# Overflow prepared in its own path, the residual before the last scatter, merged one-hot matmuls, B loaded by ScalarE, and another sequence of 27 expert rounds

## The chip, the cores and the metric

One core of a Trainium2 chip runs the whole kernel, a single program of 14302 instructions. Its engines are TensorE (PE; PEld is its weight load), VectorE (DVE), ScalarE (ACT), GpSimd (POOL) and SyncE (SP, which here only issues transfers and waits). The metric is the device time of one execution in microseconds, the median of the runs shown.

## The reference

One layer of a hybrid backbone in fp32, on 128 context tokens and 256 latent tokens of 1024 channels (384 tokens in all, three tiles of 128):

```
h = RMSNorm(x) * (1 + scale1) + shift1          # six modulation rows = SiLU(cond) @ w_ada + b_ada
p = h @ w_in                                    # S5 input 768 | Fourier input 256 | branch gates 2 x 1024
A = S5(p)                                       # 48 groups of 16 channels, 64 complex states, two directions
B = Re(DFT2(p_f))
x = x + gate1 * ((sig(gA) * (A @ w_proj_s5) + sig(gB) * (B @ w_proj_f)) @ w_out)
h = RMSNorm(x) * (1 + scale2) + shift2
x = x + gate2 * (sum over 6 of 64 experts of gate_e * (silu(h @ w1_e) * (h @ w3_e)) @ w2_e + shared(h))
y = RMSNorm(x) * final_norm_g
```

An expert's three matrices (1024 x 256, 1024 x 256, 256 x 1024) are 1 MB each. `b_re`, `b_im`, `c_re` and `c_im` are the S5 input and output matrices, discretized and raised to powers in the kernel.

## The kernel before

The program is a chain of blocks; all engines meet at the end of each.

**The front.** In the first block SP loads constants and conditioning and then streams 24 weight tiles `w_ada` of 1 MB and tiles of `w_in` through a ring of five places. ACT issues the token tiles and two position tiles (line 340 is the last), then computes SiLU of the conditioning (line 344) and the squares of the norms. POOL issues 16 loads of C (line 277), the two of B (line 280), three small ones, and then computes the powers of C (lines 313 to 317). DVE does the first norm and the S5 parameters (to line 522), waits for B and computes its powers (lines 601 to 603); after the last of them (line 638) ACT copies the modulation rows (line 358) and PE does the lag matmuls (line 478). B's load takes, per part, 48 pieces of 16 numbers (64 B) for each of 128 partitions.

**The expert stage.** Its last block runs all 64 experts once, sorted by their count of tokens. A round takes 128 slots, that is token places, cut in blocks of 32; the kinds of rounds give experts 64, 32 and 32 slots (A), 96 and 32 (B), 128 (C) or 64 and 64 (D). 27 rounds run in seven batches, three rounds in the first and four in each other, in the sequence that `PLAN` writes out by hand. Five expert slots in SBUF form a ring (`sb_W` is the fifth); SP loads the experts in the order of their places: per batch gate and up weights of rounds 0 and 1 (`gate_up`, which waits until PE has used that slot five places earlier), the down weights of round 0 (`downward`, with the like wait), gate_up 2, downward 1, gate_up 3, downward 2, downward 3.

On PE a batch is: gather the slots' tokens by a one-hot matrix S (line 1612), `hidden` of round 0 (line 1575), scatter of the two last rounds of the batch before (line 1547), and then, interleaved, for each round `slot_rows`, `hidden`, `turned` (transposes, line 1582) and `down` (line 1596), with the scatter of rounds 0 and 1 ahead of the down of rounds 2 and 3. After the last batch comes the final scatter. `slot_rows` makes three transposes of S (line 1561) and three matmuls of S with the gates, high and low half, of up to 16 blocks each (line 1563); ACT copies the transposed S (line 1651), DVE sums a slot's two gate halves (`gates`, line 1790), and PE's next `slot_rows` waits for that. DVE further forms gate times SiLU times up (line 1796), the low halves of the down results for the scatter (line 1803), which is exact in two parts, and adds the scatter's banks to the accumulator ACC (line 1741).

Experts that got more tokens than their slots hold are meant to go on in overflow batches, a loop behind a branch on a count (`batches`, line 1456). For that the last batch prepares on DVE: `rounds` (lines 1749 to 1756), 5 x `round_experts` (1758 to 1767), `round_batches` (1769 to 1774), and the first overflow batch's `Tail` (1871 to 1890) and `tail_slots` (1712 to 1721). Here the count is 0, and the loop's body does not run.

After that SP loads X (the tokens before the stage, 1.5 MB, line 1524), two gate rows (`g2b`, line 1526) and the final norm's weight; DVE adds the final scatter, multiplies by the gate and adds X, tile by tile (lines 1905 and 1906), and writes the normed output (line 1915).

## Time and profile before

| | |
|---|---|
| median of 3 runs | 1087.58 us (1085.2 to 1091.76) |
| the profiled execution | 1090.29 us, span 1088.4 us |
| mean granted TensorE clock | 0.93 |
| busy share of the span | PE 85%, PEld 46%, DVE 43%, ACT 17%, POOL 11% |
| bytes moved | 272.52 MB, 250 GB/s over the span |
| first expert load issued | 543.88 us |

Times in rows are microseconds from the start of the span. A line of a timeline has the start, the length, the engine, the line of the kernel, the operation, what is written from what is read, the shape, the number of instructions joined in the line, and in brackets how long the engine had been idle and what released it. An engine with a q (SPq, ACTq) is that engine's issuing part: its line is the issue of a transfer, not its duration. PEclk and the clock are shares of TensorE's full 2.4 GHz.

### The profile page before, as it was taken

How to read it: one execution, taken by the hardware profiler on the slowest of the kernel's cores; microseconds unless marked ns; L12 is line 12 of the kernel's file. 1: busy time of each engine (PE TensorE's matmuls, PEld its weight loads, DVE VectorE, ACT ScalarE, POOL GpSimd, SP SyncE). 2: the span in 40 equal slices, each digit the busy share in tenths (PEclk: the TensorE clock that was granted, in tenths of full speed). 3: DMA queues.
4: the chain of work that ended last, by engine and by line, in shares of the span. 5: the costliest groups of instructions: out<-in, count | busy, mean ns of one | idle time of the engine just before them, and what ended most of it. 6: DMA issues, size and time to landing. Idle time of an engine off the chain costs nothing.

```text
span 1088.4 us, 14302 instructions
## 1 busy us (share of the span) xinstructions
PE 925.6 (85%) x5613; PEld 498.3 (46%) x5613; DVE 470.2 (43%) x1103; ACT 188.3 (17%) x390; POOL 115.3 (11%) x121
## 2 busy tenths in 40 slices
PE   1719609899999899997989999999999999989883
PEld 1204208576557655443654533534535435435342
DVE  4499990125981213324532323223223232232976
ACT  3210001332003300014121111121021111111112
POOL 4599930000000000000000000000000000000000
PEclk9759859799999899997989999999999999989998
DMA  9926503602104471201099989999999999999931
GB/s 294 315 103 232 193 0 118 194 1 79 39 0 187 155 279 58 116 0 58 1 405 387 404 356 428 412 426 425 415 427 425 414 426 427 427 426 395 391 112 64
DMA packets 50364, 272.52 MB, mean 250 GB/s; under 512 B 5755, under 2 KB 14363, under 8 KB 22003
## 3 DMA queue, kind: packets, MB, share of 16 engines
q1 hardware_dynamic: 48694, 267.31, 61.0%
q10 hardware_dynamic: 768, 2.67, 0.8%
q0 software_dynamic: 832, 1.59, 0.6%
q8 instruction: 46, 0.75, 0.3%
q14 instruction: 24, 0.20, 0.0%
HBM read 268.30 MB, written 3.24 MB: 249 GB/s over the span
## 4 chain that ended last, share of the span: by engine, by line
PE 39%; DVE 4%; DMA 3%; issue 2%; ACT 1%; SPq 1%; DVEq 0%
PE bank L1575 16%; PE bank L1596 8%; PE bank L1612 7%; PE bank L1547 6%; DMA sb<-w 3%; PE bank L1582 1%; PE bank L1561 1%; ACT sb_Y L1666 0%; PE bank L1563 0%; DVE sb L1741 0%; SPq L978 0%; DVE sb L1905 0%; DVE sb L1765 0%; DVE sb L1766 0%; DVE sb L1767 0%
## 5 line engine op out<-in xcount | busy, mean ns | idle before, releaser
L1575 PE MATMUL bank<-sb 128*32 128x512 f32 (+2 forms) x1024 | 200.4, 606 | 2.2 <-DMA sb<-w 2.2
L1575 PE MATMUL bank<-sb_W,sb 128*32 128x512 f32 (+1 forms) x448 | 92.8, 644 | 13.2 <-issue 13.2
L1596 PE MATMUL bank<-sb 128*32 128x512 f32 (+2 forms) x512 | 99.3, 598 | 1.1 <-ACT sb L1661 1.1
L749 PE MATMUL bank<-early 128*128 128x384 f32 x256 | 89.7, 499 | 0.0
L1547 PE MATMUL bank<-sb_Y,sb_ST 128*128 128x512 f32 x324 | 83.7, 409 | 3.9 <-DVE sb L1741 2.2
L1575 PEld LDWEIGHTS bank<-sb 128*32 128x32 f32 (+2 forms) x1024 | 56.4, 117 | 66.1 <-issue 66.0
L1741 DVE TENSOR_TENSOR sb<-sb,bank 128x512 f32<-128x512 f32 x84 | 57.7, 687 | 65.2 <-PE bank L1547 64.5
L1612 PE MATMUL bank<-sb_S,sb_H 128*128 128x512 f32 (+1 forms) x336 | 79.3, 396 | 5.3 <-ACT sb_H L1696 4.0
L1612 PEld LDWEIGHTS bank<-sb_S,sb_H 128*128 128x128 f32 x336 | 63.7, 195 | 23.9 <-issue 9.8
L1547 PEld LDWEIGHTS bank<-sb_Y,sb_ST 128*128 128x128 f32 x324 | 55.9, 188 | 36.7 <-DVE sb L1741 14.8
L1803 DVE TENSOR_TENSOR sb_Y<-bank,sb_Y 128x512 fp32r<-128x512 f32 x54 | 37.2, 691 | 71.4 <-ACT sb_Y L1666 71.3
L749 PEld LDWEIGHTS bank<-early 128*128 128x128 f32 x256 | 46.9, 191 | 28.9
L1575 PEld LDWEIGHTS bank<-sb_W,sb 128*32 128x32 f32 (+1 forms) x448 | 27.2, 121 | 68.1 <-issue 67.9
L465 PE MATMUL bank<-early 128*128 128x384 f32 x96 | 34.6, 516 | 23.5 <-ACT early L381 23.5
L1666 ACT ACTIVATE sb_Y<-bank 128x512 fp32r<-128x512 f32 x54 | 32.3, 597 | 110.6 <-PE bank L1596 110.6
L1796 DVE SCALAR_TENSOR_TENSOR sb<-sb,bank 128x256 f32<-128x256 f32 x27 | 13.0, 480 | 85.0 <-ACT sb L1657 83.0
L1596 PE MATMUL bank<-sb_W,sb 128*32 128x512 f32 (+1 forms) x224 | 44.6, 610 | 3.2 <-ACT sb L1661 3.2
L1657 ACT ACTIVATE sb<-bank 128x256 f32<-128x256 f32 x27 | 10.4, 385 | 210.3 <-PE bank L1575 210.3
L478 PE MATMUL bank<-sb 128*32 128x128 f32 x192 | 15.1, 305 | 36.6 <-ACT sb L358 36.6
L1783 DVE COPY sb<-bank 128x512 f32<-128x512 f32 (+1 forms) x28 | 18.8, 672 | 55.9 <-PE bank L1612 55.9
L1076 PE MATMUL bank<-sb 128*128 128x512 f32 x96 | 41.5, 593 | 1.7 <-DVE sb L1226 1.7
L1596 PEld LDWEIGHTS bank<-sb 128*32 128x32 f32 (+2 forms) x512 | 26.0, 115 | 29.7 <-issue 28.1
(309 smaller groups left out, 1214.2 us busy)
## 6 DMA issues: line engine op xcount, KB each, us to landing
sb<-w SPq DMA_DIRECT2D x156, 1024.0 KB, 17.3
sb_W<-w SPq DMA_DIRECT2D x36, 1024.0 KB, 15.4
early<-w_ada SPq DMA_DIRECT2D x24, 1024.0 KB, 13.8
early<-w_in SPq DMA_DIRECT2D x12, 1024.0 KB, 10.0
sb<-w_out SPq DMA_DIRECT2D x1, 4096.0 KB, 16.0
sb<-ada_dram SPq DMA_DIRECT2D x8, 512.0 KB, 13.8
early<-w_proj_s SPq DMA_DIRECT2D x1, 2560.0 KB, 15.9
early<-w_glu SPq DMA_DIRECT2D x1, 2304.0 KB, 9.9
```

What stands on the lines that cost most here:

```text
L465: ins = nc.tensor.matmul(bank[3 + f % 2][:, 0:TOK], w_a[c][:, f * P:(f + 1) * P], hT[:, c, :], start=c == 0, stop=c == KC - 1)
L478: ins = nc.tensor.matmul(bank[kk_bank[f % 3]][32 * q:32 * q + 32, c0:c0 + P], Cpad[:, r, dq, :], BP[:, r, dq].rearrange("p s h -> p (s h)" ...
L749: ins = nc.tensor.matmul(bank[m % 2][:, 0:TOK], w[:, c, P * (m % 2):P * (m % 2) + P], hT[:, c, :], start=c == 0, stop=c == KC - 1)
L1076: ins = nc.tensor.matmul(bank[4 + n][:, :], GLT[:, m, j * P:(j + 1) * P], w_o[:, m, 512 * n:512 * n + 512], start=m == 0, stop=m == KC - 1)
L1547: ins = nc.tensor.matmul(bank[m % 2][:, :], ST[:, p, j * P:(j + 1) * P], YR[:, x, p % 2, 512 * h:512 * h + 512], start=p == ps[0] and x == ...
L1575: ins = nc.tensor.matmul(bank[2 + p % 2][c0:c0 + w, :], XT[:, c, P * p + c0:P * p + c0 + w], slot13[k][:, :, c, :], start=c == 0, stop=c = ...
L1596: ins = nc.tensor.matmul(bank[y_bank[p][h]][c0:c0 + w, :], hidT[:, f, c0:c0 + w], slot2[k][:, f, 512 * h:512 * h + 512], start=f == 0, sto ...
L1612: ins = nc.tensor.matmul(bank[c % 2][:, 0:B.slots], part[:, j, c * P:(c + 1) * P], S[:, j, 0:B.slots], start=j == 0 and x == 0, stop=j == ...
L1666: nc.scalar.activation(YR[:, 0, p % 2, 512 * h:512 * h + 512], bank[y_bank[p][h]][:, :], ACT.Copy).then_inc(y_high, 1)
L1741: tt(ACC[:, j, 512 * h:512 * h + 512], ACC[:, j, 512 * h:512 * h + 512], bank[m % 2][:, :], ALU.add).then_inc(acc_ok, 1)
L1783: nc.vector.tensor_copy(XT[:, c, 0:B.slots], bank[1][:, 0:B.slots]).then_inc(xt_dve, 1)
L1803: tt(YR[:, 1, p % 2, cols_], bank[y_bank[p][h]][:, :], Y[:, 0, p % 2, cols_], ALU.subtract).then_inc(y_low, 1)
```

## The change

- `PLAN` gives the 27 rounds another sequence; the kinds and how many there are of each stay.
- The loads of B go from POOL's queue to ACT's, behind the position tiles, and the scratch for transfers that POOL describes goes from 8192 to 4096 bytes.
- Overflow: counting (`rounds`, `round_batches`) is in batch 1, ahead of its first gates. The rest (which experts, the slots, clearing ACC) is done behind the branch, in functions that only run if the count is over 0.
- `slot_rows`: three matmuls of 160 columns take the place of three transposes and three of the gates. `sb_g` holds, per token tile, twice (16 gates and half of the identity); each matmul writes two groups of 80 columns of bank 7. ACT copies the six identity parts, and DVE's `gates` sums six numbers a slot, not two. The identity is written once, ahead of the first slots.
- Residual: X, the gate rows and the norm's weight lie in the fifth expert slot. X and the weight are loaded once that slot's last expert has been through `hidden`, the gate rows once it has been through `down`. DVE then, in the last batch, multiplies the accumulator so far by the gate and adds it to X, one tile ahead of `down(2)`, one ahead of `down(3)` and one behind it; `residual` handles the final scatter's banks alone, by half tiles.

The diff, without the overflow path's own bodies:

```diff
@@ -50,7 +50,7 @@
 N_CONST = 560
 
 KINDS = dict(A=(2, 1, 1), B=(3, 1), C=(4,), D=(2, 2))
-PLAN = ("CAB", "ADAB", "ABAD", "ABAB", "ADAB", "ADAB", "ABDC")
+PLAN = ("BBA", "ADDA", "ACAB", "ABDA", "ACAD", "ADBB", "ABAB")
...
@@ -276,8 +276,6 @@
                         for a in range(2):
                             pool.dma_start(CL[(r * 4 + q) * GH:(r * 4 + q + 1) * GH, :, a * NS:(a + 1) * NS],
                                            v[q, a]).then_inc(s_c, 16)
-                for r, name in enumerate(("b_re", "b_im")):
-                    pool.dma_start(BL[:, r], i[name][0].rearrange("d (q a) n h -> (a n) (d q) h", a=2)).then_inc(s_b, 16)
                 pool.dma_start(g1n, i["norm1_g"][0].rearrange("(p c) -> p c", c=KC)).then_inc(s_dg, 16)
...
@@ -338,6 +336,8 @@
                 x_tile(1)
                 act.dma_start(at(o_H, D), i["k_pos"][0:P, :]).then_inc(s_pos[0], 16)
                 act.dma_start(at(o_H + D, D), i["k_pos"][P:2 * P, :]).then_inc(s_pos[1], 16)
+                for r, name in enumerate(("b_re", "b_im")):
+                    act.dma_start(BL[:, r], i[name][0].rearrange("d (q a) n h -> (a n) (d q) h", a=2)).then_inc(s_b, 16)
                 act.wait_ge(zero_ok, 1)
...
+        GC, GW = 4 * 4, 4 * 4 + P // 2
...
-        sb_g = ctx.enter_context(nc.sbuf_tensor("sb_g", [P, NT * 2 * 2 * BATCH], F32R))
+        sb_g = ctx.enter_context(nc.sbuf_tensor("sb_g", [P, NT * 2 * GW], F32R))
         by_row = lambda v: v.rearrange("p (j n) -> p j n", j=NT)
-        X = by_row(at(o_V, NT * D))
-        g2b = at(o_A, 2 * D).rearrange("p (r n) -> p r n", r=2)
-        fin_g = at(o_A + 2 * D, D)
+        X = by_row(slot[RING - 1][:, 0:NT * D])
+        g2b = slot[RING - 1][:, 4 * D:6 * D].rearrange("p (r n) -> p r n", r=2)
+        fin_g = slot[RING - 1][:, 3 * D:4 * D]
...
-        gahl_t = sb_g[:, 0:48].rearrange("p (j x k) -> p j x k", j=NT, x=2)
-        gahl_b = sb_g[:, :].rearrange("p (j x k) -> p j x k", j=NT, x=2)
+        gates_id = sb_g[:, :].rearrange("p (j x c) -> p j x c", j=NT, x=2)
+        slot_bank = bank[7][:, 0:NT * 2 * GW].rearrange("p (b c) -> p b c", c=GW)
...
+                last = round_of[max(range(RING - 1, E, RING))] + 1
+                sp.wait_ge(h_mm, last)
+                sp.dma_start(X, x2_dram).then_inc(fin_in, 16)
+                sp.dma_start(fin_g, i["final_norm_g"].partition_broadcast(P)).then_inc(fin_in, 16)
+                sp.wait_ge(y1_mm, last)
+                for r in range(2):
+                    sp.dma_start(g2b[:, r, :], ada_dram[r, 5 * D:6 * D].partition_broadcast(P)).then_inc(fin_in, 16)
                 sp.wait_ge(tail_ok, 1)
                 more = sp.value_load(ids[0:1, 0:1], min_val=0, max_val=MAXT // BATCH)
                 with sp.If(more > 0):
+                    sp.wait_ge(tail_ok, 2)
...
-                sp.wait_ge(h_mm, more * 4 + N_ROUNDS)
-                sp.dma_start(X, x2_dram).then_inc(fin_in, 16)
-                for r in range(2):
-                    sp.dma_start(g2b[:, r, :], ada_dram[r, 5 * D:6 * D].partition_broadcast(P)).then_inc(fin_in, 16)
-                sp.dma_start(fin_g, i["final_norm_g"].partition_broadcast(P)).then_inc(fin_in, 16)
...
                     def slot_rows(p):
 
                         wait_last(pe, gate_col_ok, rd(1, p))
                         for j in range(NT):
-                            nc.tensor.transpose(bank[7][:, j * P:(j + 1) * P], S[:, j, P * p:P * p + P].bitcast(F32), ident)
-                        for j in range(NT):
-                            ins = nc.tensor.matmul(bank[7][:, TOK:TOK + width], S[:, j, P * p:P * p + P],
-                                                   gates_r[:, j], start=j == 0, stop=j == NT - 1)
+                            ins = nc.tensor.matmul(bank[7][:, 2 * GW * j:2 * GW * j + 2 * GW], S[:, j, P * p:P * p + P],
+                                                   sb_g[:, 2 * GW * j:2 * GW * j + 2 * GW], start=True, stop=True)
                         ins.then_inc(slot_rows_mm, 1)
...
-                        nc.scalar.activation(ST[:, p], bank[7][:, 0:TOK], ACT.Copy).then_inc(slot_rows_ok, 1)
+                        nc.scalar.activation(ST[:, p].rearrange("p (b c) -> p b c", c=P // 2), slot_bank[:, :, GC:GW], ACT.Copy
+                                             ).then_inc(slot_rows_ok, 1)
...
-                    nc.vector.tensor_copy(gahl_b[:, :, 0, 0:nk], g).then_inc(ga_high, 1)
+                    nc.vector.tensor_copy(gates_id[:, :, 0, 0:nk], g).then_inc(ga_high, 1)
...
+                def round_batches():
+
+                    step(ts(five, iota[0:1, 0:5], float(BATCH), cum_ex[0:1, E - 1:E], ALU.mult, ALU.is_lt))
+                    step(nc.vector.tensor_reduce(n_more, five, AX_X, ALU.add))
+                    nc.vector.tensor_copy(ids[:, 0:1], n_more).then_inc(tail_ok, 1)
...
+                def overflow_first():
+
+                    count = [0]
+
+                    def first_step(ins):
+                        count[0] += 1
+                        ins.then_inc(tail_step, 1)
+                        dve.wait_ge(tail_step, count[0])
+
+                    for m in range(0, MAXT, BATCH):
+                        round_experts(m, first_step)
+                    nc.vector.tensor_copy(ids[:, 1:1 + MAXT], idx_f).then_inc(tail_ok, 1)
+                    for j in range(NT):
+                        ins = nc.vector.memset(ACC[:, j], 0.0)
+                    first_step(ins)
...
+                def before_residual(j):
+
+                    if j == 0:
+                        dve.wait_ge(fin_in, 64)
+                    step(tt(ACC[:, j], ACC[:, j], g2b[:, min(j, 1)], ALU.mult))
+                    step(tt(X[:, j], X[:, j], ACC[:, j], ALU.add))
...
-                            g = gate_t[:, :, 2 * p + a] if B.tail else gate_b[:, :, 4 * p + c0 // SB]
-                            ins = nc.vector.tensor_reduce(gcol[c0:c0 + w, p:p + 1], g[c0:c0 + w], AX_X, ALU.add)
+                            k = 2 * p + a if B.tail else 4 * p + c0 // SB
+                            ins = nc.vector.tensor_reduce(gcol[c0:c0 + w, p:p + 1], slot_bank[c0:c0 + w, :, k], AX_X, ALU.add)
...
                     if not B.first:
                         add(bt, -6)
-                    if B.last:
+                    if not tail and B.b == 1:
                         rounds()
-                        round_experts(0)
+                        round_batches()
                     gates(0)
                     hidden(0)
-                    if B.last:
-                        round_experts(BATCH)
-                        round_experts(2 * BATCH)
                     gates(1)
                     hidden(1)
-                    if B.last:
-                        round_experts(3 * BATCH)
-                        round_experts(4 * BATCH)
-                        round_batches()
-                    if tail:
-                        tail.items()
-                        tail.tile(0)
                     down(0)
                     gates(2)
                     if n_rounds == 4:
                         hidden(2)
-                        if tail:
-                            tail.tile(1)
                         gates(3)
                         down(1)
-                        if tail:
-                            tail.tile(2)
-                            tail.end()
                         next_slots()
                         hidden(3)
                         add(bt, 0)
+                        if B.last:
+                            before_residual(0)
                         down(2)
+                        if B.last:
+                            before_residual(1)
                         down(3)
+                        if B.last:
+                            before_residual(2)
...
+                for x in range(2):
+                    step(ts(gates_id[:, :, x, 0:GC], ident[:, 0:GC].unsqueeze(1).to_broadcast([P, NT, GC]), 0.0, None, ALU.mult))
+                    nc.vector.tensor_copy(gates_id[:, :, x, GC:GW], ident[:, 64 * x:64 * x + 64].unsqueeze(1).to_broadcast([P, NT, P // 2]))
                 block_slots(0)
...
-                    add(n, -6, (2 * j, 2 * j + 1))
-                    if j == 0:
-                        dve.wait_ge(fin_in, 64)
-                    dve.wait_ge(acc_ok, n(12, 2 * j - 3))
-                    step(tt(ACC[:, j], ACC[:, j], g2b[:, min(j, 1)], ALU.mult))
-                    tt(X[:, j], X[:, j], ACC[:, j], ALU.add).then_inc(x3_ok, 1)
+                    for h in range(2):
+                        m, cols_ = 2 * j + h, slice(512 * h, 512 * h + 512)
+                        dve.wait_ge(scatter_mm, n(12, m - 5))
+                        tt(ACC[:, j, cols_], bank[m % 2][:, :], g2b[:, min(j, 1), cols_], ALU.mult).then_inc(acc_ok, 1)
+                        dve.wait_ge(acc_ok, n(12, m - 4))
+                        ins = tt(X[:, j, cols_], X[:, j, cols_], ACC[:, j, cols_], ALU.add)
+                    ins.then_inc(x3_ok, 1)
...
-    nc = bacc.Bacc("TRN2", target_bir_lowering=False, num_devices=1, dynamic_dma_scratch_size=8192)
+    nc = bacc.Bacc("TRN2", target_bir_lowering=False, num_devices=1, dynamic_dma_scratch_size=4096)
```

## Rows read from the trace of the kernel before

**Rows 1.** The page: the span, and the GB/s moved in its 40 slices.

```profile
span 1088.4 us, 14302 instructions
...
GB/s 294 315 103 232 193 0 118 194 1 79 39 0 187 155 279 58 116 0 58 1 405 387 404 356 428 412 426 425 415 427 425 414 426 427 427 426 395 391 112 64
```

**Rows 2.** Timeline of SP's queue (start us, us): the first expert loads.

```profile
543.88 0.84 SPq L978 DMA_DIRECT2D sb<-w  x2
```

**Rows 3.** Time windows: us, busy of PE to POOL, PEclk, DMA share, GB/s.

```profile
42.00:46.00 4.00, 0.32 (x4) 0.00 (x0) 0.00 (x0) 0.00 (x0) 3.61 (x8) 0.50 0.99 201
...
880.00:890.00 10.00, 7.57 (x57) 2.66 (x57) 3.72 (x9) 1.64 (x4) 0.00 (x0) 1.00 1.00 424
...
1030.00:1040.00 10.00, 5.22 (x26) 2.48 (x26) 9.47 (x21) 1.26 (x3) 0.00 (x0) 0.89 0.17 73
```

**Rows 4.** DMA issues: queue, count, KB each, median us to landing.

```profile
sb<-w SPq DMA_DIRECT2D x156, 1024.0 KB, 17.3
...
early<-x_prompt SPq DMA_DIRECT2D x1, 512.0 KB, 3.5
...
sb<-b_re POOLq DMA_DIRECT2D x1, 384.0 KB, 13.0
...
sb<-b_im POOLq DMA_DIRECT2D x1, 384.0 KB, 13.9
```

**Rows 5.** Timeline of DVE, from the last batch to the end.

```profile
1011.55 0.68 DVE L1763 TENSOR_TENSOR sb<-sb 1x512 f32<-1x512 f32 x1
...
1065.96 0.69 DVE L1803 TENSOR_TENSOR sb_Y<-bank,sb_Y 128x512 fp32r<-128x512 f32 x1 [1.03 <-ACT sb_Y L1666]
...
1068.01 0.69 DVE L1741 TENSOR_TENSOR sb<-sb,bank 128x512 f32<-128x512 f32 x1 [1.36 <-PE bank L1547]
...
1080.54 1.23 DVE L1906 TENSOR_TENSOR sb<-sb 128x1024 f32<-128x1024 f32 x1
```

**Rows 6.** Timeline of PE, last two batches ([idle before <-releaser]).

```profile
970.24 6.10 PE L1547 MATMUL bank<-sb_Y,sb_ST 128*128 128x512 f32 x24
...
976.27 3.64 PE L1596 MATMUL bank<-sb 128*32 128x512 f32 x32
...
1008.64 0.49 PE L1561 MATMUL bank<-sb,sb_S 128*128 128x128 f32 x3
...
1008.88 0.49 PE L1563 MATMUL bank<-sb_g,sb_S 128*128 128x32 f32 x3
...
1024.02 8.78 PE L1575 MATMUL bank<-sb 128*64 128x512 f32 x32
...
1038.02 0.90 PE L1561 MATMUL bank<-sb,sb_S 128*128 128x128 f32 x3 [4.78 <-DVE sb L1790]
...
1044.17 7.03 PE L1575 MATMUL bank<-sb 128*128 128x512 f32 x16
```

**Rows 7.** Timeline of all engines, the front.

```profile
2.14 1.19 ACTq L340 DMA_DIRECT2D early<-k_pos  x1
...
9.81 1.28 ACT L344 ACT_TABLE_LOAD   x1 [9.81 <-DMA sb<-c]
...
41.21 0.51 POOL L313 TENSOR_TENSOR sb<-sb 128x192 f32<-128x192 f32 x1 [2.87 <-ACT sb L370]
...
48.07 0.36 DVE L601 TENSOR_TENSOR sb<-sb 128x192 f32<-128x192 f32 x1 [8.74 <-DMA sb<-b_im]
...
144.05 2.00 POOL L317 TENSOR_TENSOR sb<-sb 128x768 f32<-128x768 f32 x1
...
158.95 0.96 DVE L601 TENSOR_TENSOR sb<-sb 128x768 f32<-128x768 f32 x1
...
162.80 2.54 PE L478 MATMUL bank<-sb 128*32 128x128 f32 x18 [36.57 <-ACT sb L358]
```

**Rows 8.** Source view of L1526, the two gate rows before.

```profile
DMA to landing us min/median/max: 7.8/8.5/9.2
```

**Rows 9.** Source view of L683: issue ns min/median/max of 1 MB in 1024 rows.

```profile
L683 SPq DMA_DIRECT2D early<-w_in x8: 540/658/3412, 197.4 to 276.0; - x8
```

More of the change, by code:

```diff
@@ L1454, in column_tiles, with batches @@
             return [(c, wide, *rest) for c0, w, *rest in experts for c in range(c0, c0 + w, wide)]
-        def batches(eng, body):
+        def batches(eng, body, first=None, after=None):
             for b in range(NB):
@@ L1776, in body @@
                 def body(B):
                     bt, rd = B.per_batch, B.per_round
[L1778 removed]
+                    tail = Tail(B.tail_batch) if B.tail else None
                     n_rounds = len(B.rounds)
[L1780 removed]
+                    if tail:
+                        tail.items()
+                        for j in range(NT):
+                            tail.tile(j)
+                        tail.end()
+                        dve.wait_ge(pm_ok, B.tail_batch(1, 1))
+                        tail_slots(bt(1, 1))
```

45 lines of the change are left out of this document (21 added, 24 removed).

## The prediction

> **What bounds the kernel now.** The profiled execution took 1090.29 us for a span of 1088.4 [rows 1]; 1.9 us lie around the span, and it is 2.7 us above the median, 1087.58, to which I apply every difference worked out below.
>
> I read the time windows first, then the DMA issues, then the timelines of PE and DVE at the end, then the front. From 543.88 on [rows 2] the expert stage is a stream of loads: a window in its middle has a DMA share of 1.00 at 424 GB/s while PE is busy for 7.57 of 10 us [rows 3]. 192 loads of 1 MB (64 experts by 3; [rows 4] has 156 of them) are 201.3 MB, at the 427 GB/s of the page's slices [rows 1] 471 us; the stream ends near 1031.7, as the window from 1030 has a share of only 0.17 [rows 3]. Until then work on an engine counts only if it holds the stream up. After it come 57 us in which nothing is loaded but the residual's inputs, and there each step counts whole. In that end, and in the last batch ahead of it, DVE prepares the overflow: 25 look-up steps and 15 of the tiles, each of 512 columns and some 0.7 us [rows 5], 28 us, with counting and slots some 34. PE waits for it: 4.78 us for the gates at 1038.02, and before that its 32 matmuls of a round took 8.78 us at a lowered clock where a later round took 7.03 [rows 6].
>
> The front is a chain too. DVE waits 8.74 us for b_im, so from 39.3, and starts B's powers at 48.07 [rows 7]. PE's lag matmuls at 162.80 have waited 36.57 us for what follows those powers [rows 7], so what moves this chain moves the end one for one.
>
> **The change, part by part.**
>
> *Overflow.* In batch 1 only counting stays, eleven short steps of DVE ahead of the first gates, none wider than a look-up's 0.68 [rows 5]: at most 7.5 us, and as an estimate 3, being an eighth as wide. PE idles for a quarter of a window of that stream [rows 3], so I price it at 0; without that cover it costs 3. In the last batch 34 us of DVE go. The overflow body does not run here in either kernel.
>
> *Sequence of rounds.* The kinds and counts stay, so the bytes and the end of the stream stay at 1031.7; other stalls at batch borders may move it by 5 us either way. What changes is what lies behind the last gate and up load: SP issues gate_up(3), downward(2), downward(3), so there remain 5 down loads (3 experts, then 2), where there were 3. One takes 2.456 us (1 MB at 427 GB/s): the last gate and up weights land at 1031.7 - 12.3 = 1019.4, and with 2 us for the signal and the round before, hidden(3) starts at 1021.4. With the clock lowered, since PE waited for the load, it takes 8.8, not 7.0, and ends at 1030.2; before, it ended at 1051.2 [rows 6]. Then scatter 6.1 and down(2) 3.6 [rows 6]: 1039.9.
>
> *Residual.* SP now loads X and the norm weight after the hidden of round 25 and the two gate rows (512 KB each) after its down, 1039.9. None of this stands ahead of an expert load in SP's order, and X and the norm weight, 2 MB or 4.9 us behind the last load, are in by 1037. For the gate rows the nearest prices are 3.5 us for 512 KB on an idle stream [rows 4] and 9.2 for this pair behind the 1.5 MB of X [rows 8]. I take 3.5, with 1.2 for the second's bytes at 427 GB/s and, as an estimate, 1.1 for the wake-up and two issues: 5.8, so 1045.7; at 9.2 it is 1049.1. DVE stands in that wait with the down parts of rounds 2 and 3 queued behind it, and PE's final scatter waits for these. Then: first tile 2 x 1.23 = 2.5 (1048.2), two halves of 0.69 [rows 5] (1049.6), second tile 2.5 (1052.1), two halves (1053.5). Final scatter: 1.4 for the first bank [rows 5], six banks of 4 matmuls. At full clock these are 1.0 each, and DVE's third tile and residual (2.5, then 4 x 0.69 = 2.8 a tile) end at 1064.4; at half the clock (1.2 of 2.4 GHz), as PE's transposes after its 4.78 us wait took 0.90, not 0.49 [rows 6], in a window whose mean granted clock is 0.89 [rows 3], they are 2.0 each and end at 1066.2. PE will have waited 10 us: I take 1066.2. From the last residual add to the end of the span it was 6.6 us (1081.8 to 1088.4) [rows 1, 5]: 1072.8. So the stage gives 1088.4 - 1072.8 = **-15.6**.
>
> *Merged matmuls.* Three of 32 columns took 0.49 in the trace's overlapping line, with a pitch of 0.11, and so did the three transposes [rows 6]. Three of 160 columns lie between that pitch (-0.33 a round) and a 512-column one, 6.10 / 24 = 0.25 [rows 6] (+0.03). Nearest is a third of the latter way, -0.24: 27 rounds are -6.5 on PE. But the loads set the pace there, so I take 0; the ends are -3, if half of it comes through, and +1 (27 x 0.03). Six values in gates() rather than two, and ACT's strided copy, are under 0.2 a round beside the loads: 0. Filling the identities is some 1 us on DVE when the stage starts, before the first weights have landed (17.3 us [rows 4]): 0.
>
> *B on ScalarE's queue.* POOL spends 13.0 and 13.9 us on landing b_re and b_im and DVE waits for the second. On ACT's queue they are issued at 3.33, right after k_pos (2.14 + 1.19) [rows 7], and could be in before DVE needs them. What is that worth? At most 8.74. But DVE runs beside POOL's powers: POOL's 768-column step takes 2.00 and DVE's 0.96 when alone [rows 7]; of 8.74 us more beside POOL at 2.0 a step, 4.4 steps of 0.96 = 4.2 are gained. Between 4.2 and 8.7 I take 6. The price is on ACT: B is 2 x 6144 pieces of 64 B, and ACT's first computation (9.81) stands behind both issues. No row shows such a load on ACT. If the issue needs no queue room, ACT loses nothing: -6. If ACT is free once b_re is through (3.3 + 13.0 = 16.3), it starts 7 later, DVE's first stage ends at 46.3, and DVE gains only 1.7; POOL's powers, which wait for ACT's copies (41.21), come 7 later too and keep slowing DVE. Nearest to POOL's own landing, I take this: gain and delay cancel, **0**. Both ends beyond it are rivals below. The smaller scratch costs nothing visible: POOL's remaining loads are c's 48 KB and a few rows.
>
> Sum: -15.6 + 0 = **1072.0 us** against the median.
>
> **The rivals.**
>
> *1. B's pieces take turns with the big rows (about 1086).* The transport is full in the front: share 0.99 at 42 to 46, with only 201 GB/s while b_im's pieces are in flight [rows 3]. If ACT is held until both loads are through, at POOL's landings, 3.3 + 13.0 + 13.9 = 30.2, it starts 20 us late: DVE's first stage ends at 59.7, 11.6 after 48.07, and POOL's powers start 20 late. Between these I take +14: 1072 + 14 = 1086. For it: the two landings. Against it: what POOL's queue takes includes the time its own engine needs to write the pieces. The Trainium skill, page "DMA: Bandwidth & Descriptors", section "Queues, rings and completion order", says that each DMA engine goes round its queues by packets; by that rule B's small packets wait their turn behind packets of the weight stream, and the hold is this rival's, not the forecast's. The drop to 201 GB/s agrees with mixed packets; that ACT is held, no row shows.
>
> *2. ACT is held by the count of pieces (about 1102, slower).* The worst issue of 1024 rows held SP for 3.41 us [rows 9]. B has 12 times as many pieces: 12 x 3.41 = 41 us, so ACT is free at 44, 34 late. DVE starts its powers 24 later, POOL 34: I take +30, 1102. It decides once the front is 21 us late, for then the 15.6 are gone and 5.4 more. Against it: the median of those issues was 0.66, and it was the queue behind a filled stream that held the worst.
>
> *3. The stage gives half back (about 1080).* The gate rows land at 9.2 us, the final scatter stays slow in all, and a new stall at a batch border takes 4: -15.6 + 3.4 + 4 = -8. For it: DVE and PE both hang on two short loads. Against it: the loads then have the transport to themselves.
>
> *4. The change does not do what it says,* that is, the overflow path runs: then the time would rise by whole batches. Hidden needs just the matmuls of 27 rounds and the choice of experts is the data's, so nothing but 0.01 is left for it.
>
> **How the numbers follow.** A measurement tells about 0.5%, 5.4 us, from no change: faster is below 1082.1, slower above 1093.0. Forecast 0.50 (1066 to 1078; the front's bounds of -6 and +6), rival 3 0.12, rival 1 0.22, rival 2 0.13, rest (rival 4 in it) 0.03. Faster: 0.50 + 0.12 + 0.04 of rival 1's lower edge = 0.66. Slower: 0.13 + 0.01 = 0.14. Same: 0.20. The range goes down to 1063 (-15.6, the front at -6 and the merged matmuls at -3) and up to 1090, so that it leaves rival 2, rival 1's upper edge and little else out.
>
> **What would show it.** Right: in the last batch no look-ups on DVE, hidden(3) ending near 1030 less the front's shift, a DVE wait of some 5 to 9 us for the gate rows, the last residual add 6.6 before the end; ACT's first computation no later than 17 and PE's lag matmuls near 163. Wrong: ACT's first computation at 30 or later and the lag matmuls past 175 (rivals 1 and 2), a stream that ends past 1036 less that shift, or rounds whose merged matmuls take over 0.7 us.

## The result: no gain, two shifts of opposite sign

The changed kernel takes 1092.07 us (median of 20 runs, 1085.92 to 1108.48) against 1090.2 of the kernel before in as many; the ratio is 1.0026, interval 1.0014 to 1.0038. One run of each kernel was a slow one (1108.48 here, 3194.91 before), and the ratio leaves those out. The changed kernel's profiled execution has a span of 1090.9 us against 1088.4 [rows 1]. I had predicted 1072.0 and a range up to 1090.

Start with where the two kernels stand at the same landmark. SP issues the first expert load, in the timeline of its queue in the changed kernel, 15.4 us later than before [rows 2]:

```profile
559.27 0.84 SPq L978 DMA_DIRECT2D sb<-w  x2
...
1035.02 0.43 SPq L1518 DMA_DIRECT2D sb_W<-x_dram  x1
...
1054.57 0.80 SPq L1522 DMA_DIRECT2D sb_W<-ada_dram  x2
```

From there to the end it is 1090.9 - 559.27 = 531.6 us, before 1088.4 - 543.88 = 544.5. So the expert stage gained 12.9 us, of the 15.6 that I had summed up, and the front lost 15.4, for which I had put 0. The front after, in the timeline of all engines:

```profile
3.29 0.53 ACTq L340 DMA_DIRECT2D sb<-b_re  x1
3.85 27.90 ACTq L340 DMA_DIRECT2D sb<-b_im  x1
5.26 49.39 SPq L257 DMA_DIRECT2D early<-w_ada  x8
...
31.84 1.28 ACT L344 ACT_TABLE_LOAD   x1 [31.84 <-issue]
...
58.28 0.35 DVE L601 TENSOR_TENSOR sb<-sb 128x192 f32<-128x192 f32 x1
...
60.25 0.51 POOL L311 TENSOR_TENSOR sb<-sb 128x192 f32<-128x192 f32 x1 [38.19 <-ACT sb L370]
...
176.69 6.95 PE L478 MATMUL bank<-sb 128*32 128x128 f32 x64 [42.91 <-ACT sb L358]
```

The second of B's loads holds ACT's queue for 27.9 us, and the computation that stands behind it starts at 31.84 instead of 9.81 [rows 7]. DVE no longer waits for B, but it gets to B's powers 10.2 us later (58.28, before 48.07), and the lag matmuls start 13.9 later (176.69, before 162.80) [rows 7].

The end after, on PE, counted in the text from the first expert load so that the front drops out:

```profile
1036.57 8.36 PE L1574 MATMUL bank<-sb 128*32 128x512 f32 x64 [2.81 <-issue]
1044.86 6.08 PE L1551 MATMUL bank<-sb_Y,sb_ST 128*128 128x512 f32 x24
...
1055.50 3.64 PE L1595 MATMUL bank<-sb 128*32 128x512 f32 x32 [0.56 <-ACT sb L1661]
1067.68 3.78 PE L1551 MATMUL bank<-sb_Y,sb_ST 128*128 128x512 f32 x8 [8.54 <-DVE sb_Y L1841]
1074.57 6.52 PE L1551 MATMUL bank<-sb_Y,sb_ST 128*128 128x512 f32 x16 [3.11 <-DVE sb L1933]
```

The last hidden ends at 485.7 (1044.93 - 559.27); before it was 507.3 (1051.2 - 543.88) [rows 6]. Those 21.6 us are the sequence and the missing overflow work together. But PE then stands for 8.54 us ahead of the final scatter and 3.11 inside it, where it stood 1.49 and 1.90 before, in PE's timeline:

```profile
1066.78 4.10 PE L1547 MATMUL bank<-sb_Y,sb_ST 128*128 128x512 f32 x16 [1.49 <-DVE sb_Y L1803]
1072.78 2.14 PE L1547 MATMUL bank<-sb_Y,sb_ST 128*128 128x512 f32 x8 [1.90 <-DVE sb L1741]
```

The timeline of DVE in the changed kernel shows what both waits are for:

```profile
1060.03 1.23 DVE L1805 TENSOR_TENSOR sb<-sb,sb_W 128x1024 f32<-128x1024 f32 x1 [8.37 <-DMA sb_W<-ada_dram]
...
1073.83 0.69 DVE L1933 TENSOR_TENSOR sb<-bank,sb_W 128x512 f32<-128x512 f32 x1 [3.88 <-issue]
...
1083.59 0.69 DVE L1935 TENSOR_TENSOR sb_W<-sb_W,sb 128x512 f32<-128x512 f32 x1
```

The gate rows are issued at 1054.57, behind the down of the fifth slot's last expert, and DVE waits 8.37 us for them with two rounds' down parts behind it. A second stop of 3.88 us, with nothing that the profile shows to wait for, lies at the branch on the overflow count.

### The profile page after: what moved, and what is told of

Its sections match the earlier page's. It is cut to its first block and busy times, and to the rows that moved or that the text cites. A ratio compares the mean times of both kernels' runs of the same rounds, so it can differ in the third digit from the quotient of the medians.

```text
span 1090.9 us, 14089 instructions
## 1 busy us (share of the span) xinstructions
PE 915.7 (84%) x5532; PEld 488.7 (45%) x5532; DVE 447.1 (41%) x1059; ACT 186.2 (17%) x390; POOL 116.8 (11%) x119
## 3 DMA queue, kind: packets, MB, share of 16 engines
q10 hardware_dynamic: 13088, 3.46, 1.6%
## 5 line engine op out<-in xcount | busy, mean ns | idle before, releaser
L1574 PE MATMUL bank<-sb 128*32 128x512 f32 (+2 forms) x1152 | 189.6, 610 | 6.1 <-DMA sb<-w 3.3
L1595 PE MATMUL bank<-sb 128*32 128x512 f32 (+2 forms) x576 | 94.7, 596 | 4.7 <-ACT sb L1661 4.7
L1551 PE MATMUL bank<-sb_Y,sb_ST 128*128 128x512 f32 x324 | 87.4, 423 | 12.1 <-DVE sb_Y L1841 8.5
L1574 PEld LDWEIGHTS bank<-sb 128*32 128x32 f32 (+2 forms) x1152 | 53.1, 116 | 94.6 <-issue 93.6
L1574 PE MATMUL bank<-sb_W,sb 128*32 128x512 f32 (+2 forms) x320 | 89.3, 615 | 4.5 <-DMA sb<-w 4.5
L1551 PEld LDWEIGHTS bank<-sb_Y,sb_ST 128*128 128x128 f32 x324 | 59.0, 197 | 46.2 <-issue 20.3
L1739 DVE TENSOR_TENSOR sb<-sb,bank 128x512 f32<-128x512 f32 x78 | 53.6, 687 | 63.5 <-PE bank L1551 62.9
L478 PE MATMUL bank<-sb 128*32 128x128 f32 x192 | 15.6, 313 | 42.9 <-ACT sb L358 42.9
L1595 PE MATMUL bank<-sb_W,sb 128*32 128x512 f32 (+2 forms) x160 | 43.6, 596 | 2.1 <-ACT sb L1661 2.1
L1595 PEld LDWEIGHTS bank<-sb 128*32 128x32 f32 (+2 forms) x576 | 24.8, 113 | 44.0 <-issue 36.8
L602 DVE TENSOR_TENSOR sb<-sb 128x192 f32<-128x192 f32 (+2 forms) x32 | 40.7, 1272 | 0.0
```

What stands on the lines that cost most here:

```text
L602: step(tt(dest, src[x1], ar, ALU.mult))
L1551: ins = nc.tensor.matmul(bank[m % 2][:, :], ST[:, p, j * P:(j + 1) * P], YR[:, x, p % 2, 512 * h:512 * h + 512], start=p == ps[0] and x == ...
L1574: ins = nc.tensor.matmul(bank[2 + p % 2][c0:c0 + w, :], XT[:, c, P * p + c0:P * p + c0 + w], slot13[k][:, :, c, :], start=c == 0, stop=c = ...
L1595: ins = nc.tensor.matmul(bank[y_bank[p][h]][c0:c0 + w, :], hidT[:, f, c0:c0 + w], slot2[k][:, f, 512 * h:512 * h + 512], start=f == 0, sto ...
L1739: tt(ACC[:, j, 512 * h:512 * h + 512], ACC[:, j, 512 * h:512 * h + 512], bank[m % 2][:, :], ALU.add).then_inc(acc_ok, 1)
```

## The experiments

My theory after this result: B's loads on ACT's queue hold ACT while their pieces take turns with the weight stream, and that alone costs the front what the stage gains. Its rivals: a hold by the count of pieces; other parts of the change in the front; and, for the stage, which of its four edits made the gain. Each kernel was run beside the kernel before on the chip that it ran on; e5 to e8 ran on another chip than the rest, where the kernel before took 1089.82 us, against 1089.31 and 1089.81. Every kernel from e3 on, e4 and e11 aside, has B on SP's queue. Lag matmuls, first expert load and the stage (from that load to the span's end) are from the profiles.

| run | median us | ratio to before (interval) | lag matmuls | first expert load | stage |
|---|---|---|---|---|---|
| before | 1090.2 | | 162.80 | 543.88 | 544.5 |
| changed | 1092.07 | 1.0026 (1.0014 to 1.0038) | 176.69 | 559.27 | 531.6 |
| e1 before, B on ACT | 1102.61 | 1.0125 (1.0108 to 1.0142) | 176.12 | 557.27 | 543.6 |
| e2 changed, B on POOL | 1082.62 | 0.9938 (0.992 to 0.9956) | 167.20 | 548.27 | 533.8 |
| e3 changed, B on SP | 1054.19 | 0.9675 (0.9659 to 0.9691) | 140.26 | 522.21 | 531.8 |
| e4 B on ACT, alone | 1077.62 (one run) | | 163.36 | 543.10 | 532.7 |
| e5 e3, gate rows early | 1050.49 | 0.9611 (0.9554 to 0.9669) | 140.17 | 521.15 | 526.8 |
| e6 e5, other order | 1043.67 | 0.9597 (0.9559 to 0.9634) | 133.21 | 511.27 | 528.0 |
| e7 e3, old sequence | 1053.3 | 0.9674 (0.9627 to 0.972) | 140.31 | 520.48 | 532.3 |
| e8 e3, work put back | 1054.07 | 0.9681 (0.9656 to 0.9707) | 136.53 | 517.00 | 533.6 |
| e9 e6, C's powers held | 1037.31 | 0.9523 (0.9484 to 0.9561) | 123.29 | 507.43 | 528.0 |
| e10 e6, old sequence | 1053.72 | 0.9671 (0.9628 to 0.9714) | 133.97 | 515.13 | 536.2 |
| e11 before, new sequence | 1077.38 | 0.9889 (0.9849 to 0.9928) | 162.12 | 541.67 | 531.0 |
| e12 e3, old slot rows | 1050.84 | 0.9656 (0.9613 to 0.97) | 136.63 | 514.56 | 530.9 |

Changed, e2, e3 and e4 share one stage, and their profiles put it at 531.6 to 533.8, so a difference of some 2 us between two single profiles tells nothing. The front spreads more: e3, e5 to e8, e10 and e12 share one, and its lag matmuls start between 133.2 and 140.3. So the totals of these runs are compared less than their stages.

### The front: e1 to e4

**e1**, the kernel before with this part alone:

```diff
-                for r, name in enumerate(("b_re", "b_im")):
-                    pool.dma_start(BL[:, r], i[name][0].rearrange("d (q a) n h -> (a n) (d q) h", a=2)).then_inc(s_b, 16)
...
                 act.dma_start(at(o_H + D, D), i["k_pos"][P:2 * P, :]).then_inc(s_pos[1], 16)
+                for r, name in enumerate(("b_re", "b_im")):
+                    act.dma_start(BL[:, r], i[name][0].rearrange("d (q a) n h -> (a n) (d q) h", a=2)).then_inc(s_b, 16)
```

> The kernel before with one part of the change alone: B's two loads on ScalarE's queue behind the position tiles. Theory (the front gives the stage's gain back): ScalarE starts at 31 to 32 instead of 9.8, the lag matmuls at 176 to 177 instead of 162.8, the first expert load 15 us later, and the whole is 15 us slower than before, about 1105. Rival (most of the front's shift comes from something else in the change, or is taken up before the expert stage): under 5 us slower.

Measured: 13.3 us slower, the lag matmuls at 176.12, the expert stage as before. In its timeline the front of the changed kernel is there whole:

```profile
3.88 27.21 ACTq L340 DMA_DIRECT2D sb<-b_im  x1
...
31.18 1.28 ACT L344 ACT_TABLE_LOAD   x1 [31.18 <-issue]
```

So this one edit makes the front's loss, and the rival that something else in the change makes it falls.

**e2** moves the two loads back to POOL's queue, with a scratch of 7168 bytes, as much as fits beside the wider `sb_g`:

```diff
+                for r, name in enumerate(("b_re", "b_im")):
+                    pool.dma_start(BL[:, r], i[name][0].rearrange("d (q a) n h -> (a n) (d q) h", a=2)).then_inc(s_b, 16)
                 pool.dma_start(g1n, i["norm1_g"][0].rearrange("(p c) -> p c", c=KC)).then_inc(s_dg, 16)
...
-                for r, name in enumerate(("b_re", "b_im")):
-                    act.dma_start(BL[:, r], i[name][0].rearrange("d (q a) n h -> (a n) (d q) h", a=2)).then_inc(s_b, 16)
...
-    nc = bacc.Bacc("TRN2", target_bir_lowering=False, num_devices=1, dynamic_dma_scratch_size=4096)
+    nc = bacc.Bacc("TRN2", target_bir_lowering=False, num_devices=1, dynamic_dma_scratch_size=7168)
```

> The changed kernel with B's loads back on GpSimd's queue (scratch of 7168 bytes, as much as fits). Theory: the front is that of before (lag matmuls near 163, first expert load near 544), the expert stage keeps its 531.6 us against 544.5, so 13 us faster than before, about 1077, and some 15 faster than the changed kernel. Rival (the stage's gain depends on the later start, or the smaller scratch slows the front): less than 8 us faster than before.

Measured: 6.7 us faster than before, under the 13 expected: the rival's sign, but by the front and not by the stage, which kept its gain (533.8). In the timeline of POOL:

```profile
37.23 0.55 POOL L282 DMA_DIRECT2D sb<-norm_g  x1
48.74 0.84 POOL L283 DMA_DIRECT2D sb<-d_skip  x1 [10.96 <-issue]
49.68 0.52 POOL L313 TENSOR_TENSOR sb<-sb 128x192 f32<-128x192 f32 x1
```

POOL stops 10.96 us more, ahead of a 3 KB load that went straight through before, and C's powers start at 49.68 instead of 41.21 [rows 7]. That the scratch makes this stop, e1 and the changed kernel show: in both B is on ACT's queue, and POOL comes to that load with 8192 bytes of scratch in e1 and 4096 in the changed kernel. From their POOL timelines, in this order:

```profile
11.19 0.86 POOL L281 DMA_DIRECT2D sb<-d_skip  x1
```

```profile
21.19 0.86 POOL L281 DMA_DIRECT2D sb<-d_skip  x1 [9.97 <-issue]
```

The scratch that I had priced at nothing has a price wherever B stays on POOL's queue; the rest of the change takes the room it had.

**e3** puts them on SP's queue, ahead of the 24 `w_ada` tiles.

```diff
+                for r, name in enumerate(("b_re", "b_im")):
+                    sp.dma_start(BL[:, r], i[name][0].rearrange("d (q a) n h -> (a n) (d q) h", a=2)).then_inc(s_b, 16)
                 for n in range(len(items)):
                     load(n)
```

> The changed kernel with B's loads on SyncE's queue, ahead of the stream of w_ada. Theory: ScalarE is free at once (its first computation near 10), B is in by 20 to 32, the VectorE starts B's powers at 39 without a wait, and w_ada comes 10 to 28 us later, which those powers hide: lag matmuls at 156 to 160, total 1070 to 1076. Rival (w_ada's delay ends last): the modulation rows hold up the lag matmuls and the total is 1085 or more.

Measured: 1054.19, better than the theory's best, and the lag matmuls at 140.26 instead of 156 to 160. **e4** leaves B on ACT's queue, but SP waits for it ahead of its first weight tile:

```diff
+                sp.wait_ge(s_b, 32)
                 for n in range(len(items)):
                     load(n)
```

> The changed kernel, B on ScalarE's queue, but SyncE issues no w_ada before B has landed, so B's pieces meet only the small loads and the token tiles. If the hold comes from taking turns with the weight stream, ScalarE's issue of b_im is over in 10 to 18 us instead of 27.9. If it comes from the count of pieces (2.3 ns for each of 12288), it again takes 25 to 28 us.

Measured: the issue of b_im takes 14.60 us. From the timelines of SP in e3 and of ACT in e4, in this order:

```profile
5.66 12.55 SPq L268 DMA_DIRECT2D sb<-b_im  x1
```

```profile
3.77 14.60 ACTq L341 DMA_DIRECT2D sb<-b_im  x1
```

Without the weight stream the same pieces are out in half the time, on either queue, so it is turn-taking and not the count of pieces alone: 12 x 3.41 = 41 us, my rival 2, was nowhere near. The page's table of queues shows what takes turns. In the changed kernel:

```profile
q1 hardware_dynamic: 48694, 267.31, 60.4%
q10 hardware_dynamic: 13088, 3.46, 1.6%
q0 software_dynamic: 608, 0.80, 0.3%
```

ACT's queue (q10) has 13088 packets; e3, with B elsewhere, has 768 there. The 12320 more are B's 12288 pieces of 64 B and a few besides, one packet each. On SP's queue (q1) e3 has as many more, 61014. POOL's queue (q0) carried the same bytes in 832 - 608 = 224 packets. The Trainium skill, page "DMA: Bandwidth & Descriptors", section "Queues, rings and completion order", has each DMA engine go round its queues packet by packet; by that rule every 64 B piece lets a packet of the weight stream pass first, and the trace agrees: 27.9 us beside the stream, 14.6 without it. The trace's records of single packets show the turns themselves. In the changed kernel, from 12 to 28 us, 713 pieces of B went beside 567 packets of 8 KB of the stream. The stream's first five tiles, 640 such packets that fill its ring of five places, were out at 29.67; by then 1265 of B's 12288 pieces had gone, and the other 11023 went in the next 6.4 us. So most of B waited for a pause of the stream, and ACT came free 2 us after that pause began (31.75; in e1 the pause began at 29.08 and ACT came free at 31.09).

e3 also shows that B's arrival was worth more than I allowed. DVE starts the powers at 36.39 there, 11.7 us sooner than before, and the lag matmuls come 22.5 sooner. I had written that of 8.74 us at most 8.7 come through. What else changed is which engine leads. Before, POOL starts its powers 6.9 us ahead of DVE [rows 7]; in e3 DVE leads by 7.2, and its powers take 103.0 us from first to last, before 113.8. From e3's timelines of DVE and of POOL, in this order:

```profile
36.39 0.35 DVE L601 TENSOR_TENSOR sb<-sb 128x192 f32<-128x192 f32 x1
```

```profile
43.59 0.51 POOL L313 TENSOR_TENSOR sb<-sb 128x192 f32<-128x192 f32 x1 [24.37 <-ACT sb L370]
```

### The stage: e7, e8, e11, e12

**e11** is the kernel before with the new `PLAN` alone:

```diff
-PLAN = ("CAB", "ADAB", "ABAD", "ABAB", "ADAB", "ADAB", "ABDC")
+PLAN = ("BBA", "ADDA", "ACAB", "ABDA", "ACAD", "ADBB", "ABAB")
```

and **e7** is e3 with the same two lines the other way round.

> The kernel before with the new sequence of rounds alone. If the preparation of the overflow is what holds up the last rounds, the sequence alone gives 0 to 3 us from the first expert load to the end (542 to 545 instead of 544.5). If the sequence alone makes the gain, 532 to 535.

> The kernel with B on SyncE's queue and the old sequence of the 27 rounds, all else as changed. Theory by my sum (the sequence moves the last hidden ahead by having five down loads behind its weights rather than three): the last hidden ends 5 us later, 3 to 6 us slower than 1054. Rival (the gain is all the overflow's and the residual's): the same within 2 us.

Measured: the sequence alone makes the whole gain (531.0), and without it the rest makes as much (532.3, within the spread of the changed stage). The two are not additive. In e7 the last hidden moves as the theory has it, by 8.2 us rather than 5, but the total as the rival has it. In e11 DVE's overflow work is still there and PE still waits for it, in its timeline:

```profile
1020.44 0.90 PE L1561 MATMUL bank<-sb,sb_S 128*128 128x128 f32 x3 [6.65 <-DVE sb L1790]
...
1034.62 6.08 PE L1547 MATMUL bank<-sb_Y,sb_ST 128*128 128x512 f32 x24
1051.11 4.12 PE L1547 MATMUL bank<-sb_Y,sb_ST 128*128 128x512 f32 x16 [2.21 <-DVE sb_Y L1803]
```

so its last hidden ends at 493.0 from the first load, 7.3 later than in the changed kernel; yet its final scatter starts at 509.4, against 508.4. In e7 the last hidden ends at 493.5 and the final scatter starts at 509.1. What the last hidden gains in the changed kernel, 7 to 8 us over either, is all but lost in the wait for the gate rows: the final scatter starts some 1 us earlier. In e7 that wait is not there: the timeline of its queue and of DVE, in this order, show the rows issued at 1006.74 and used at 1020.45 with no idle time.

```profile
1006.74 0.80 SPq L1522 DMA_DIRECT2D sb_W<-ada_dram  x2
```

```profile
1019.85 0.69 DVE L1739 TENSOR_TENSOR sb<-sb,bank 128x512 f32<-128x512 f32 x1 [0.24 <-PE bank L1551]
1020.45 1.22 DVE L1805 TENSOR_TENSOR sb<-sb,sb_W 128x1024 f32<-128x1024 f32 x1
```

The reason lies in the code: the residual waits for the fifth slot's last expert, place 59. With the old last batch, ABDC, its eight experts are places 56 to 63, and 59 is in its second round; with ABAB there are ten, 54 to 63, and 59 is in the third. The new sequence takes 8 us off the last hidden and hands them to the residual's loads.

**e8** puts DVE's load back into the last batch of e3:

```diff
+                    work = lambda n: [round_experts(BATCH * k, step) for k in range(n)] if not tail and B.last else None
+                    work(1)
                     gates(0)
                     hidden(0)
+                    work(2)
...
+                    work(3)
                     down(0)
```

and one more on each side of `gates(3)` and `down(1)`.

> The kernel with B on SyncE's queue and, in the last batch, VectorE's load of the old overflow preparation put back as eight look-ups of 3.5 us at the places where it stood (their results are not used). Theory (the preparation held up PE): PE waits again for the gates of rounds 2 and 3, and the total rises by 5 to 10 us over 1054. Rival (with the new sequence PE waits for its weights there anyway): under 2 us.

Measured: 533.6, 1.8 more than e3, which is within the spread of that stage, and the same total (1054.07), not the 5 to 10 us more of the theory. PE does wait again, 4.56 us for the gates of round 2, and its last hidden ends 4.4 later (489.7 against 485.3), but the gate rows' wait takes most of it up. In the timeline of its PE:

```profile
992.87 0.93 PE L1562 MATMUL bank<-sb_g,sb_S 128*128 128x160 f32 x3 [4.56 <-DVE sb L1828]
...
1029.60 3.78 PE L1551 MATMUL bank<-sb_Y,sb_ST 128*128 128x512 f32 x8 [8.65 <-DVE sb_Y L1841]
```

**e12** has three transposes and three narrow matmuls again, with ACT's copy and DVE's two-number sum to match:

```diff
                         for j in range(NT):
-                            ins = nc.tensor.matmul(bank[7][:, 2 * GW * j:2 * GW * j + 2 * GW], S[:, j, P * p:P * p + P],
-                                                   sb_g[:, 2 * GW * j:2 * GW * j + 2 * GW], start=True, stop=True)
+                            nc.tensor.transpose(bank[7][:, j * P:(j + 1) * P], S[:, j, P * p:P * p + P].bitcast(F32), ident)
+                        for j in range(NT):
+                            ins = nc.tensor.matmul(bank[7][:, TOK:TOK + 2 * GC], S[:, j, P * p:P * p + P],
+                                                   gates_id[:, j, :, 0:GC], start=j == 0, stop=j == NT - 1)
```

> The kernel with B on SyncE's queue, with the three transposes and three narrow matmuls of the gates again. By my price (merged matmuls hidden under the loads): within 3 us of 531.8 from the first expert load to the end, and 0.55 to 0.75 us instead of 0.46 to 0.57 on PE per round. Rival (they delay the loads through the chain of gates): 5 us or more longer.

Measured: 530.9, against 531.8 with the merged ones: no difference that two profiles could tell. On PE a round's slot rows took 0.74 us from the first start to the last end (971.26 to 972.00), the merged three 0.46 to 0.57.

### Towards a better kernel: e5, e6, e10, e9

**e5** swaps what lies where in the fifth slot, so that only the third tile of X and the norm's weight wait for the down:

```diff
-        X = by_row(slot[RING - 1][:, 0:NT * D])
-        g2b = slot[RING - 1][:, 4 * D:6 * D].rearrange("p (r n) -> p r n", r=2)
-        fin_g = slot[RING - 1][:, 3 * D:4 * D]
+        X = by_row(slot[RING - 1][:, 2 * D:5 * D])
+        g2b = slot[RING - 1][:, 0:2 * D].rearrange("p (r n) -> p r n", r=2)
+        fin_g = slot[RING - 1][:, 5 * D:6 * D]
...
                 sp.wait_ge(h_mm, last)
-                sp.dma_start(X, x2_dram).then_inc(fin_in, 16)
-                sp.dma_start(fin_g, i["final_norm_g"].partition_broadcast(P)).then_inc(fin_in, 16)
-                sp.wait_ge(y1_mm, last)
                 for r in range(2):
                     sp.dma_start(g2b[:, r, :], ada_dram[r, 5 * D:6 * D].partition_broadcast(P)).then_inc(fin_in, 16)
+                sp.dma_start(X[:, 0:2], x2_dram[:, 0:2]).then_inc(fin_in, 16)
+                sp.wait_ge(y1_mm, last)
+                sp.dma_start(X[:, 2], x2_dram[:, 2]).then_inc(s_b, 16)
+                sp.dma_start(fin_g, i["final_norm_g"].partition_broadcast(P)).then_inc(s_b, 16)
```

> The kernel with B on SyncE's queue, and in the fifth slot the gate rows lie where the gate and up weights were, with X from there on: gate rows and two tiles of X are loaded behind the last hidden of that slot, the third tile of X and the norm weight behind its last down. Theory (VectorE's wait of 8.4 us for the gate rows holds up the final scatter): the wait is gone, the final scatter starts 5 to 7 us earlier, and the total falls from 1054 to 1047 to 1050. Rival (the loads hide the wait, or it turns up at X): within 2 us of 1054.

Measured: DVE's wait, 8.68 us in e3, is 0.97, and the stage is 5.0 us shorter (526.8). The direction is the theory's, the size a little less: counted from the first load, the final scatter starts 3.4 us earlier (504.9 against 508.3), not 5 to 7, and the total went down by 3.7, with runs from 1039.86 to 1051.41.

**e6** also changes DVE's order:

```diff
+                        down(2)
                         if B.last:
                             before_residual(0)
-                        down(2)
+                        down(3)
                         if B.last:
                             before_residual(1)
-                        down(3)
-                        if B.last:
-                            before_residual(2)
...
                 residual(1)
+                before_residual(2)
                 output(0)
```

> As the run before it, and VectorE does the low halves of rounds 2 and 3 ahead of the two products and sums that stood before them, and the third tile's product and sum behind the branch on the overflow count. Theory (the branch costs VectorE the 3.9 us in which it stood idle, and PE's final scatter waits for it): branch and products run beside PE's final scatter and its wait for round 3's down, 3 to 6 us less than the run before it. Rival (VectorE's work in sum sets the end, whatever its order): within 1.5 us of it.

Measured: by the total the theory seems right (-6.8), but the stage is not shorter (528.0). The total is the front's: its lag matmuls start at 133.21 where e3's and e5's start at 140.2, with the same front. The rival holds; the order does nothing, and the idle 3.9 us at the branch stay. In e8 DVE stood only 1.63 there, and the timeline names PE's scatter as what ended it. What makes it 3.9 is open, but the traces have a hint: in each of the ten with a stop of 3.9 to 4.2 us, one packet of 8 KB on the instruction queue (q14) starts 1.9 to 2.1 us before DVE goes on, and in e8 none falls into the stop. That points to the fetch of the code behind the branch; no run tests it.

**e10** is e6 with the old sequence, by e7's edit.

> The kernel of the run with gate rows early and the other order, with the old sequence of rounds. With the residual's wait out of the way the sequence should be worth what it moves the last hidden by: 5 to 8 us longer from the first expert load to the end (533 to 536 instead of 528). If the sequence gives nothing even so, within 2 us of 528.

Measured: 536.2, 8.2 us longer, and the last hidden ends 7.6 later (494.5 against 486.9). With the gate rows out of the way the sequence is worth what it moves.

**e9** tests why the front moves by 7 us between profiles of one front. The seven profiles go by DVE's lead over POOL at their first powers: with a lead of 7.1 to 7.3 us (e3, e5, e7) the lag matmuls start at 140.2 to 140.3, with 8.2 to 8.3 (e8, e12) at 136.5 to 136.6, with 8.6 (e6, e10) at 133.2 to 134.0. In these traces DVE and POOL take each other's steps one for one while both do powers, and DVE's 768-column step, 0.96 alone [rows 7], takes 2.1 to 2.4 beside POOL's. e9 is e6 with POOL holding its widest level:

```diff
                     w = max(m, 1)
+                    if m == 4:
+                        pool.wait_ge(bp_ok, 2)
```

In e6's DVE timeline and then in e9's:

```profile
127.81 2.22 DVE L602 TENSOR_TENSOR sb<-sb 128x768 f32<-128x768 f32 x1
130.07 2.11 DVE L603 TENSOR_TENSOR sb<-sb 128x768 f32<-128x768 f32 x1
```

```profile
120.32 0.95 DVE L604 TENSOR_TENSOR sb<-sb 128x768 f32<-128x768 f32 x1
121.30 0.96 DVE L605 TENSOR_TENSOR sb<-sb 128x768 f32<-128x768 f32 x1
```

> The kernel of the run with gate rows early and the other order (B on SyncE's queue), and GpSimd holds its last level of C's powers, 24 steps of 768 columns, until VectorE has done B's powers. Theory (the two engines take each other's steps one for one, so what ends the front is how many of VectorE's wide steps are done beside GpSimd's wide ones): VectorE's last dozen steps take 0.96 us instead of 2.1 to 2.6, the lag matmuls start 10 to 16 us earlier (117 to 125), GpSimd ends near 162 to 166, still inside the block, and the total is 1028 to 1036. Rival (VectorE's wide steps are slow for another reason, or GpSimd then ends the block): within 4 us of 1043.

Measured: 1037.31 (1036.83 to 1038.66), the best here, 4.8% under the kernel before, and just outside both ranges: the theory's time was up to 1036, the rival's from 1039. The lag matmuls start at 123.29, as the theory has it. That is 10 us sooner than e6, of which 3.8 reach the expert stage, because, as the rival has it, POOL now ends the block:

```profile
123.29 5.87 PE L480 MATMUL bank<-sb 128*32 128x128 f32 x64 [15.40 <-ACT sb L360]
...
159.63 1.80 POOL L319 TENSOR_TENSOR sb<-sb 128x768 f32<-128x768 f32 x1
...
162.05 6.06 PE L706 MATMUL bank<-sb,early 128*48 128x128 f32 x28 [8.01 <-PEq L239]
```

The Trainium skill, page "SBUF — State Buffer", section "SBUF: two separate sides", says that the two engines share a port pair that one step locks whole; the steps' times agree with it: DVE's 2.11 and 2.22 us in e6, beside POOL's steps, against 0.95 and 0.96 in e9, without them.

## Why the prediction was wrong, step by step

- **B on ScalarE's queue: the step that failed.** I took the hold of ACT to end with b_re, at 16.3, by POOL's landing, and let gain and delay cancel at 0. It ended with the issue of b_im, at 31.8, and the front lost 13.9 us up to the lag matmuls and 15.4 up to the first expert load. That is rival 1, which had 30.2 for ACT, +14 for the front and a chance of 0.22. The evidence for it stood in the prediction, beside the rule that spoke for it: two loads through a full transport take their turns. I held against it that POOL's landings include the time POOL needs to write the pieces; the trace of before has that time, 2.25 us of 13.0 and 2.22 of 13.9 (POOL's line 280), far too little to take one of the two away. That the rival's 30.2 came so near is in part luck: it adds up POOL's two landings, while ACT came free 2 us after the stream's pause began at 29.67. (Rival 2's powers would start 25 us later by its own terms, not 24; nothing hangs on that.)
- **What B's arrival is worth** was mis-sized too, as 6 of 8.74 us. Runs show -22.5 for 11.7 sooner (e3) and +13.9 for 10.2 later: which engine leads, and so how the wide steps of the two fall together, decides, and one wide step of DVE beside a wide one of POOL costs some 1.2 us more than alone (2.2 - 0.96).
- **Sequence: right in its own place.** The last hidden was to start at 1021.4 - 543.9 = 477.5 from the first load and end at 486.3: 477.3 and 485.7. It took the missing overflow work too: with the sequence alone (e11) it ends at 493.0.
- **Residual: right up to the branch.** Gate rows predicted to land at 501.8 from the first load: DVE goes on at 500.8. Final scatter at half the clock: 1.9 us a bank in its first two (3.78 for two, at a granted clock of 0.50), against the 2.0 priced. Missing was the 3.88 us stop behind the third tile's sum, a term that the sum did not have and that makes most of the 2.7 by which the stage fell short. And I counted the wait for the gate rows, but did not see that the new sequence itself causes it.
- **Overflow and merged matmuls.** The two matmul forms differ by nothing that two profiles could tell (0.9 us), as priced. One bound was worked out wrong: three steps of 0.25 in place of six of 0.11 are +0.09 a round, not +0.03, and a third of the way there is -0.19, not -0.24; the forecast took 0 and does not hang on it. The overflow's removal is worth at most some 2 us beside the other edits (1.8 in e8, one pair of profiles), since the gate rows' wait comes after it anyway; I had counted it and the sequence as one and never asked what each is worth without the other.
- **The baseline.** The median of three runs was 1087.58, that of twenty 1090.2. That alone puts the forecast 2.6 too low. With the front's 15.4 and the stage's missing 2.7 it makes 20.7, of the 20.1 us by which the median missed. The profiles close: 15.4 - 12.9 = 2.5 = 1090.9 - 1088.4, where 13.9 of the 15.4 are there at the lag matmuls and 1.5 come between them and the first load.

## What to carry to other kernels

A transfer in small pieces costs the queue that issues it as long as its packets take turns with what the other queues stream; put it where nothing waits behind it, and ahead of the stream, not beside it. When a chain is moved ahead, look for what it will meet next: here 8 us won by a better order of rounds were handed to a load whose buffer the same order freed later. Compare kernels from landmark to landmark: two parts of this change of 13 and 15 us cancel in the total and would have passed for an edit without effect.

## What the runs showed of the hardware that I had not expected

- The same 64 B pieces are one packet each on the queues of ACT and SP (12320 packets more) and 224 packets on POOL's. Beside a stream of 8 KB packets they went about one for one (713 beside 567 from 12 to 28 us), and in its pause 11023 in 6.4 us.
- DVE's and POOL's vector steps hold each other up one for one, so that DVE's powers 11.7 us sooner made the lag matmuls 22.5 sooner (e3), and a lead longer by 1.4 us goes with an end 7 us sooner between two executions of one front (140 to 133). A DVE step of 192 columns, 0.36 alone, takes 1.5 to 2.0 beside POOL's of 768, nearly as much as a wide one.
- DVE stood for 3.9 to 4.2 us at a branch whose body does not run, in ten traces; the cause is open.
